# Inverting the heads' triangular matrices: 8x8 blocks solved row by row with three merging levels, in place of 2x2 blocks with five

## The reference

```python
def step(state, inp):
    r_t, w_t, k_t, v_t, a_t, b_t = inp
    sa = jnp.einsum('bhvk,bhk->bhv', state, a_t)
    state = state * w_t[:, :, None, :] + sa[..., None] * b_t[:, :, None, :] + v_t[..., None] * k_t[:, :, None, :]
    y = jnp.einsum('bhvk,bhk->bhv', state, r_t)
    return state, y

y_f, bonus_f = direction(0)      # each calls wkv7_scan over the 512 tokens
y_b, bonus_b = direction(1)
y = y_f + y_b                    # then a norm per head, lnx_w, lnx_b, the gate g and w_o
```

## Time and profile before

| engine | busy us in the whole span | share |
|---|---|---|
| PE | 3033.1 | 93% |
| PEld | 2411.6 | 74% |
| DVE (VectorE) | 1839.9 | 57% |
| ACT (ScalarE) | 1393.7 | 43% |
| POOL (GpSimd) | 669.0 | 21% |

### The profile page before, as it was taken

One profiled execution on the slowest core, in us unless ns is written; L12 is line 12 of the kernel. 1 busy time (PEld: TensorE's weight loads), 2 busy tenths in 40 slices (PEclk: granted clock), 3 DMA queues, 4 the chain that ended last, 5 costly groups with the idle time before them and its releaser, 6 DMA issues. The chain is left out here.

```text
span 3252.6 us, 59877 instructions
## 1 busy us (share of the span) xinstructions
PE 3033.1 (93%) x25454; PEld 2411.6 (74%) x25454; DVE 1839.9 (57%) x2665; ACT 1393.7 (43%) x2369; POOL 669.0 (21%) x542
## 2 busy tenths in 40 slices
PE   8989999999978999999989999889689989799999
PEld 6757788887746788887658888767577777588887
DVE  6665543445665543446665736474476867457464
ACT  6555422235455422234464424345465655244242
POOL 1000311211000310212001101143275746011010
PEclk9989999999989999999999999989899999799999
DMA  4101333332101323332013323335311111133232
GB/s 148 52 2 65 104 97 94 94 96 82 56 5 62 96 96 97 93 98 78 1 53 92 109 85 101 100 104 194 131 49 30 49 36 45 44 98 109 79 99 83
DMA packets 82344, 260.72 MB, mean 80 GB/s; under 512 B 9632, under 2 KB 13216, under 8 KB 81824
## 3 DMA queue, kind: packets, MB, share of 16 engines
q1 hardware_dynamic: 71424, 235.39, 23.0%
q10 hardware_dynamic: 10656, 21.50, 1.8%
HBM read 235.89 MB, written 20.97 MB: 79 GB/s over the span
## 5 line engine op out<-in xcount | busy, mean ns | idle before, releaser
L1698 DVE TENSOR_TENSOR mlp_w_lo<-mlp_ring,mlp_w_hi 128x1024 fp32r<-128x1024 f32 (+1 forms) x211 | 251.7, 1193 | 573.0 <-ACT mlp_w_hi L1675 572.9
L1675 ACT ACTIVATE mlp_w_hi<-mlp_ring 128x1024 fp32r<-128x1024 f32 (+1 forms) x211 | 213.3, 1011 | 642.2 <-PE ps L1636 637.3
L1698 DVE TENSOR_TENSOR ffn_w_lo<-ffn_ring,ffn_w_hi 128x1024 fp32r<-128x1024 f32 (+3 forms) x172 | 224.2, 1304 | 438.2 <-ACT ffn_w_hi L1675 438.2
L1675 ACT ACTIVATE ffn_w_hi<-ffn_ring 128x1024 fp32r<-128x1024 f32 (+3 forms) x172 | 187.3, 1089 | 480.8 <-PE ps L1636 476.0
L1635 PE MATMUL ps<-mlp_more_parts,mlp_w_hi 128*128 128x512 f32 x952 | 372.3, 391 | 0.0
L1634 PE MATMUL ps<-tiles_parts,mlp_w_hi 128*128 128x512 f32 x832 | 329.7, 396 | 1.1 <-issue 1.1
L1634 PE MATMUL ps<-ffn_x_parts,ffn_w_hi 128*128 128x512 f32 x792 | 312.6, 395 | 18.2 <-DVE ffn_x_parts L2413 14.2
L1636 PE MATMUL ps<-tiles_parts,mlp_w_lo 128*128 128x512 f32 x832 | 327.7, 394 | 0.0
L1634 PE MATMUL ps<-mlp_more_parts,mlp_w_hi 128*128 128x512 f32 x760 | 304.7, 401 | 19.1 <-DVE mlp_w_lo L1698 10.8
L1635 PE MATMUL ps<-ffn_x_parts,ffn_w_hi 128*128 128x512 f32 x792 | 310.3, 392 | 0.0
L1636 PE MATMUL ps<-ffn_x_parts,ffn_w_lo 128*128 128x512 f32 x792 | 310.2, 392 | 0.0
(11 more groups left out here) (504 smaller groups left out, 6188.5 us busy)
## 6 DMA issues: line engine op xcount, KB each, us to landing
ffn_ring<-in_w_ffn_up SPq DMA_DIRECT2D x88, 512.0 KB, 3.6
mlp_ring<-in_w_up SPq DMA_DIRECT2D x64, 512.0 KB, 3.6
mlp_ring<-in_w_down SPq DMA_DIRECT2D x64, 512.0 KB, 3.6
rwkv_keep<-ffn_ring ACTq DMA_DIRECT2D x64, 256.0 KB, 2.5
sq<-rwkv_keep SPq DMA_DIRECT2D x64, 256.0 KB, 3.0
ffn_ring<-in_w_ffn_down SPq DMA_DIRECT2D x16, 768.0 KB, 4.2
in_ring<-in_w_in SPq DMA_DIRECT2D x22, 512.0 KB, 3.6
mlp_ring<-in_w_in SPq DMA_DIRECT2D x22, 512.0 KB, 3.6
```

What stands on the lines that cost most here:

```text
L1675: nc.scalar.activation(w.w_hi[:, n % SPLIT, 0:width], w.ring[:, n % RING, 0:width], ACT.Copy).then_inc(s["w_hi_ready"], 1)
L1698: nc.vector.tensor_tensor(w.w_lo[:, n % SPLIT, 0:width], w.ring[:, n % RING, 0:width], w.w_hi[:, n % SPLIT, 0:width].bitcast(F32), ALU.sub ...
```

## The change

The 2x2 starting blocks become 8x8 starting blocks, and the levels go from five to three, so 24 blocks of merging are left of 40. The 8x8 diagonal blocks of all 16 instances are gathered by eight matmuls with selection matrices into one tile of 16 x 8 columns (`base_out`), to which VectorE adds the identity (`first_terms`). Then six rows are solved one after the other: one matmul that spreads a row (`row_out`), a product (terms) and a sum (X8) on VectorE (`row`); each waits for the one before. GpSimd expands the result into X (`x0`), now one instruction per token tile but only after the last row. `gram_r` and `mr` go from FRONT to between these steps, and `x0t` from FRONT to SEED. The 40 beats of MERGE are spread over the 24 blocks. GpSimd's first six `part`s go ahead of `x0`. The table of masks grows from 640 to 2504 columns.

```diff
-RW_LEVELS = 5
+RW_BASE = 8
+RW_LEVELS = 3
...
-    return [(MERGE + n, *block) for n, block in enumerate(order)]
+    beats = APPLY - MERGE
+    return [(range(MERGE + beats * n // len(order), MERGE + beats * (n + 1) // len(order)), *block) for n, block in enumerate(order)]
...
+                def base_out(c):
+                    pe.wait_ge(s["ma_ready"], 8 * c + 8)
+                    for b in range(RW_BASE):
+                        own = M0[:, :, :, b * RW_BASE:(b + 1) * RW_BASE].rearrange("p t i n -> p (t i) n")
+                        mm = nc.tensor.matmul(base_scores(), square_of("take", b), own, start=b == 0, stop=b == RW_BASE - 1, skip_group_check=True)
+                    mm.then_inc(s["base_out"], 1)
+
+                def row_out(c, n):
+                    if n == 1:
+                        pe.wait_ge(s["first_terms"], c + 1)
+                    else:
+                        pe.wait_ge(s["row_added"], ROWS * c + n - 1)
+                    nc.tensor.matmul(base_row(n), square_of("row", n), X8[:, :, 0:n], start=True, stop=True, skip_group_check=True).then_inc(s["row_out"], 1)
...
-                    nc.gpsimd.tensor_tensor(X[:, t, :, :], M0[:, t, :, :], spread(mask("pair"), 4), ALU.mult).then_inc(s["paired"], 1)
-
                 def x0(c, t):
-                    pool.wait_ge(s["paired"], 4 * c + t + 1)
-                    nc.gpsimd.tensor_tensor(X[:, t, :, :], X[:, t, :, :], spread(mask("eye"), 4), ALU.add).then_inc(s["x0_ready"], 1)
+                    pool.wait_ge(s["row_added"], ROWS * (c + 1))
...
+                    nc.gpsimd.tensor_tensor(X[:, t, :, :].rearrange("p i (b n) -> p i b n", b=RW_BASE), solved, own, ALU.mult).then_inc(s["x0_ready"], 1)
...
+                def first_terms(c):
+                    dve.wait_ge(s["base_out"], c + 1)
+                    eye = spread(masks[:, RMASKS["eye"]:RMASKS["eye"] + RW_BASE], 4 * NT)
+                    nc.vector.tensor_tensor(X8[:], base_scores(), eye, ALU.add).then_inc(s["first_terms"], 1)
+
+                def row(c, n):
+                    if n == 1:
+                        dve.wait_ge(s["first_terms"], c + 1)
+                    dve.wait_ge(s["row_out"], ROWS * c + n)
+                    factor = X8[:, :, n:n + 1].broadcast_to([P, 4 * NT, n])
+                    nc.vector.tensor_tensor(terms[:, :, 0:n], base_row(n), factor, ALU.mult).then_inc(s["row_terms"], 1)
+                    dve.wait_ge(s["row_terms"], ROWS * c + n)
+                    nc.vector.tensor_tensor(X8[:, :, 0:n], X8[:, :, 0:n], terms[:, :, 0:n], ALU.add).then_inc(s["row_added"], 1)
```

More of the change, by code:

```diff
@@ L72 @@
 BANDS2_W = 3 * P
-RMASKS, RMASKS_W = columns(("after", HD), ("before", HD), ("upto", HD), ("pair", HD), ("eye", HD), ("merge", RW_LEVELS * HD))
+RMASKS, RMASKS_W = columns(("after", HD), ("before", HD), ("upto", HD), ("own", HD), ("eye", RW_BASE), ("merge", RW_LEVELS * HD), ("take", RW_BASE * P), ("row", RW_BASE * P))
 def constants():
@@ L2931, in _ @@
                             scan_beat(i - 1, FRONT + 4 * t + 2 + n)
+                    if old:
+                        gram_r(i - 1, 0)
+                    if main:
+                        base_out(i)
+                    if old:
+                        gram_r(i - 1, 1)
                     if oldest:
@@ L3081, in _ @@
                             inner_taken(i, t, level)
-                        beats(k)
+                        for k in ks:
+                            beats(k)
                     for n, work in enumerate((wt_taken, u0_taken)):
@@ L3138, in _ @@
                             part(i, t, level)
+                    for t in range(NT):
+                        if main:
+                            x0(i, t)
                     parts = iter(parts[PARTS_EARLY:])
-                    for k, _, _, second in merge_order():
+                    for ks, _, _, second in merge_order():
                         more = None if second else next(parts, None)
@@ L3331, in _ @@
-                    for k, t, level, second in merge_order():
+                        for k in range(FRONT + 4 * t, FRONT + 4 * t + 4):
+                            beats(k)
+                    if old:
+                        mr(i - 1, 0)
+                    if main:
+                        first_terms(i)
+                    if old:
+                        mr(i - 1, 1)
+                    if main:
+                        r_late(i, 0)
+                    beats(MIDDLE)
+                    if main:
+                        row(i, 1)
@@ new lines, in _ @@
+                    if old:
+                        mr(i - 1, 2)
+                    if main:
+                        bonus_in(i)
+                    beats(MIDDLE + 1)
+                    if main:
+                        row(i, 2)
+                    if old:
+                        mr(i - 1, 3)
+                    for pair in range(2):
+                        if main:
+                            row(i, 3 + pair)
+                        if main and pair == 0:
+                            r_late(i, 1)
+                        beats(MIDDLE + 2 + pair)
@@ L3332, in _ @@
+                    if main:
+                        row(i, 5)
+                        row(i, 6)
+                        bonus(i)
+                    beats(MIDDLE + 4)
+                    beats(MIDDLE + 5)
+                    for t in range(NT):
+                        if main:
+                            x0t(i, t)
+                        beats(SEED + t)
+                    for ks, t, level, second in merge_order():
                         if main and second and level < RW_LEVELS - 1:
```

90 lines of the change are left out of this document (48 added, 42 removed).

## The result

The changed kernel took 3277.88 us (median of 4 runs, 3272.29 to 3279.71), the kernel before 3254.03 us beside it (4 runs, 3250.06 to 3256.2): 1.0076 times the time of before, 95% interval 1.0062 to 1.009. It is slower, as forecast, but by 24 us and not by 9.5. By the profiled executions, on which the working rested, it is 3272.29 against 3254.34 us: +18.0. The profiled execution of the changed kernel is the shortest of its four (the others took 3276.94 to 3279.71 us), so of the 24 us only these 18 can be followed in a trace here.

What follows compares the result with a forecast made beforehand. TensorE and VectorE were taken to pace each other, VectorE becoming MERGE's bound. FRONT -2.5, MIDDLE +9.4, SEED +1.4, MERGE -4.8 and 1.0 given back make +2.5 per full iteration, +9.5 total: 3264 us (stated range 3232 to 3290, own 3253 to 3277).

Steps and rivals of the forecast that it cites:

- FRONT, 9.5 forecast: First stage of an iteration: without four `gram_r` and their mask waits it falls from 12.0 to 9.5 us.
- the stall of 1.43: In FRONT's first scores: a 1.43 us stall not tied to a semaphore, assumed to stay.
- MIDDLE: Stage with gathering and rows: TensorE's work grows from 6.8 to 12.9 us, sixth row ends at 23.5, stage at 24.3.
- the line that was drawn: VectorE's small row operations in MIDDLE: 155 ns at 16 columns to 242 at 96; 3.0 us in all with signals.
- the step that failed: SEED, between MIDDLE and MERGE: first seed at 26.5, last ends at 30.7, so merging starts 8.3 us later.
- The cover of `x0` is gone: Before SEED: GpSimd's expansion, formerly within FRONT, starts at 23.6; VectorE reaches the first transpose only at 26.0.
- MERGE, 20.8 forecast: Merging stage: 24 blocks of 40 remain, VectorE with 20.0 us left becomes the bound, from 25.6 to 20.8 us.
- The give-back of 1.0: GpSimd idle in MIDDLE shortens VectorE's heads_R, so 1.0 us per iteration comes off the added time.
- The sum: Whole stage: +2.5 us in each of iterations 2 to 6, -3.0 for 0, 1 and 7 together; total +9.5.
- That TensorE's content decides: Whole iteration: TensorE loses 7.7 us, gains 4.0, so each iteration is 3.7 shorter; 3224 us, chance 0.27.
- That the rows aren't covered: MIDDLE: each of six rows costs 0.6 us more, 29 us on top of the forecast; 3293 us, chance 0.13.
- The wash: Whole iteration: unexplained stalls shrink with TensorE's instructions and GpSimd's silence helps VectorE by 2, not 1; 3255 us, chance 0.15.

Runs made afterwards that it cites:

- e7: The kernel before with only `gram_r` and its mask moved out of FRONT into MIDDLE, old inversion kept: 3263.37 us, ratio 1.003 to the kernel before.
- e2: The changed kernel without its six row steps, the start value being the gathered block plus the identity: 3270.74 us, ratio 1.0058 to the kernel before.
- e5: The changed kernel with `x0t` of tiles 0 and 1 ahead of the second running sum, the others ahead of the floor and state step: 3261.84 us.
- e4: The changed kernel with the eight gathering matmuls issued once more before the seeds, into PSUM nobody reads: 3269.42 us, ratio 1.0056 to the kernel before.
- e6: The kernel before with only the four transposes of the start value moved into SEED, old inversion kept: 3300.64 us, ratio 1.0143 to the kernel before.
- e9: e5 with the last two VectorE operations of the oldest tile's tail moved from MERGE to APPLY: 3258.84 us, ratio 1.0026 to the kernel before.
- e12: e9 with `gram_r` and its mask back in FRONT and the oldest tile's whole tail in APPLY: 3241.94 us, ratio 0.9969 to the kernel before.
- e3: The changed kernel with GpSimd filling X early from M0, not from the solved rows: 3302.07 us, ratio 1.0162 to the kernel before.

## Why the prediction was right in sign and short in size

**FRONT, 9.5 forecast.** 9.7: right. In place of the stall of 1.43 that was kept stands the turn's wait for heads_y, 1.06. Whether it is the same stall was not shown; e7 prices the move of `gram_r` at 0.3%.

**MIDDLE.** The gathering was priced at 2.2 and took 2.0 (2576.31 to 2578.29). The row matmuls, priced at 0.3, are 0.22 to 0.36 apart from their followers. Idle times of 0.9 and 0.7 us in front of rows 3 and 6 were forecast and did not come; one of 0.52 in front of `zv` did. VectorE's small operations are near the line that was drawn, 155 to 242 ns plus some 20, over the whole stage (busy, mean ns, idle before):

```profile
L3233 DVE TENSOR_TENSOR heads_terms<-ps,heads_X 128x96 f32<-128x96 f32 x8 | 2.1, 258 | 4.5 <-PE ps L2794 4.5
L3233 DVE TENSOR_TENSOR heads_terms<-ps,heads_X 128x16 f32<-128x16 f32 x8 | 1.4, 177 | 0.0
```

The sixth row was due at 23.5 and ended at 23.0, the first seed at 26.5 and came at 26.0. That the rows mostly ride along between other work is what e2 shows: without them the first seed comes 1.4 sooner.

**SEED: the step that failed.** The prediction put the seeds' lateness down to "The cover of `x0` is gone". The place was right, the cause half wrong: its own next words, the transpose behind `bonus`, a scan step and the running sum, are what it waits for, as GpSimd's first instruction was done before VectorE asked, and e5 takes 1.3 us of the lateness away without touching GpSimd. Its size was right only at the full clock: 4.2 us from the first seed to the last were forecast, and iterations 2 and 3 have 4.1. In 4, 5 and 6 they are 5.8 to 6.1. The prediction held the wait (2.29 us) and not what it does: TensorE's granted clock drops in some iterations, SEED of iteration 4 runs at 0.54, and in iteration 4 the low clock lasts to 2602.6, into MERGE. That is a missing term of some 2 us in three full iterations, and it has part in iteration 1, which was +3.3 where a small loss in MIDDLE and a gain of 8 in MERGE were expected.

The Trainium skill, "TensorE: Matmul & The Clock Gate", section "HAM oscillation — how this bites in real kernels", describes a related loss: short bursts of matmuls between longer waits for DMA, each burst starting at the lower clock. The case here is milder, as TensorE was busy 13.5 of the 16.3 us of MIDDLE and waited 2.29, and yet the clock fell in three of five iterations. e4 and e6 agree in kind: with more work in the gap the clock stays up at the seeds, and with such a gap in the kernel before it falls there too.

**MERGE, 20.8 forecast.** 20.9, bound by VectorE as argued: 24 blocks go with 17.2 us of TensorE (15.6 at the full clock, in iteration 3), three reciprocals stand at the start, and TensorE waits for heads_U, 17.5 us in the stage against 12.1. e9 and e12 confirm the bound by relief, down to 20. One thing the prediction held fixed did move: the tail's last three operations (L3293, L3296, L3300) have medians of 1.48, 1.11 and 1.19 us beside GpSimd in the changed kernel's MERGE, where they took 1.01, 0.86 and 0.84 before. In e12's APPLY, with GpSimd silent, they take 0.75, 0.75 and 0.69.

**The give-back of 1.0.** heads_R does take 0.68 now, in place of up to 1.16, but in a stretch that TensorE sets. That it therefore did not reach the path is argued and was not tested.

**The sum.** Iterations 2 to 6 came to +20.6 us in place of +12.5: the clock in three of them is about 6, the give-back up to 5 if none of it came, and the remainder would be smaller gains. Iteration by iteration it is +3.4 and +2.1 in 2 and 3, where the clock held, near the +2.5 forecast, and +5.9, +4.5 and +4.7 in 4, 5 and 6, where it fell. So the low clock is most of what these iterations exceed the forecast by. Iterations 0, 1 and 7 came to -1.3 in place of -3 (-1.7, +3.3, -2.9), and the tail end of the stage to -1.2. The measured 3277.88 lies inside the stated range and 1 us above the forecast's own, 3253 to 3277. That one was drawn too narrow for its own terms: base_out from 1.8 to 4.2 is -3 to +16 us over eight iterations, the small operations from 1.5 to 5.3 are -12 to +18, and it gives -3 to +13 and -10 to +12 without a working.

**The rivals.** That TensorE's content decides fell: TensorE has less to do and waits more. That the rows aren't covered had a time 15 us above the measured one (3293), about as far off as the forecast was below it (14), but not its mechanism: TensorE hardly waits between the rows. The wash fell with the give-back.

## What to carry to other kernels

When a change shortens one stage and adds steps before it, price both the steps and the place where the new result is taken up. Here the shorter merging gave 1.5%, what the new inversion adds took 1.4% back, and the order of a few unchanged instructions took another 0.8%, which turned a change that would otherwise be about even into a loss. The last part is the cheapest to win: an operation on which the busiest engine waits belongs ahead of work in its queue that can wait. And a wait of TensorE can cost more than its length: price what stands behind it at the lower clock as well, and leave a piece of work (here `gram_r`) in front of a wait where there is one.

## What the runs showed of the hardware that was not expected

- TensorE's clock: behind a wait of 2.29 us the seeds' six matmuls took 2.89 us in iteration 4 and 1.95 in iteration 3, with the same work in front; over SEED of iteration 4 the mean granted clock was 0.54, nearly all of it the lower level of 1.2 GHz (0.50). With eight more matmuls in the gap (e4) it was high over the seeds of all five full iterations.
- VectorE beside GpSimd: a sum of 80 columns from two SBUF operands took 1.27 us in place of 0.25, ending 0.10 after GpSimd's 1.26 us instruction that started 0.09 before it, in six of the eight iterations of e3. A product of 16 columns with one operand in PSUM took no longer beside GpSimd.
- A pair of 128-column matmuls that make one fp32 product, with new 128x128 weights, takes 0.25 us in a row of eight (`base_out` of the changed kernel, 1.98 us from its start to the next row's).
